# Block 1 attention: VectorE takes the rotations of heads 0 and 1 ahead of recurrences 6 and 7, and the row maxima of head 0 between the two

## The reference, cut to what matters

```
proj = x @ w_in                      # -> x_rnn, g_rnn, q_lat, kv_lat, k_rope, gate_a, gate_b
h_t  = a_t * h_(t-1) + u_t           # RG-LRU over the conv of x_rnn; a, u from its gates
y_rnn = gelu(g_rnn) * h
q    = rms_norm(q_lat) @ w_uq        # 16 heads x (64 plain + 32 rotated)
k, v = rms_norm(kv_lat) @ w_ukv      # k: 64 plain, and 32 rotated, shared by all heads
s    = causal(q k^T / sqrt(96)); p = softmax(s); y_mla = p v
merged = sigmoid(gate_a) * y_rnn + sigmoid(gate_b) * y_mla
x = layer_norm(ALPHA * x + merged @ w_out)
x = layer_norm(ALPHA * x + conv_ffn(x))
```

## Time and profile before

| | us |
|---|---|
| median of 3 runs | 3032.64 |
| lowest, highest | 3029.26, 3034.89 |
| the profiled execution, its own time | 3036.06 |
| its span in the trace | 3034.3 |

### The profile page before, as it was taken

One profiled execution on the slowest core, in us unless ns is written; L12 is line 12 of the kernel. 1 busy time (PEld: TensorE's weight loads), 2 busy tenths in 40 slices (PEclk: granted clock), 3 DMA queues, 4 the chain that ended last, 5 costly groups with the idle time before them and its releaser, 6 DMA issues. The chain is left out here.

```text
span 3034.3 us, 36255 instructions
## 1 busy us (share of the span) xinstructions
PE 2866.3 (94%) x12934; PEld 2256.6 (74%) x12934; DVE 1720.1 (57%) x2416; ACT 1069.9 (35%) x1851; POOL 1540.4 (51%) x929
## 2 busy tenths in 40 slices
PE   8989999999999899999999999889999799899996
PEld 6768787888876687878888876668667566687764
DVE  6865645443137756454442256566777475677775
ACT  3533323221025333332220122534555314444563
POOL 4543356666764533376666654565225253672241
PEclk9999999999999899999999989999999899899998
DMA  4211122333332211123233222125983321246942
GB/s 152 72 63 53 53 75 78 96 96 97 97 97 71 70 56 56 56 77 97 97 97 104 71 91 68 41 91 188 341 320 118 115 70 56 70 169 229 361 166 83
DMA packets 87035, 338.28 MB, mean 111 GB/s; under 512 B 19953, under 2 KB 22769, under 8 KB 77937
## 3 DMA queue, kind: packets, MB, share of 16 engines
q1 hardware_dynamic: 67744, 303.33, 29.4%
q0 software_dynamic: 17280, 26.26, 2.5%
q10 hardware_dynamic: 1872, 6.82, 0.6%
HBM read 371.98 MB, written 30.41 MB: 133 GB/s over the span
## 5 line engine op out<-in xcount | busy, mean ns | idle before, releaser
L179 POOL TENSOR_SCALAR wh<-ring 128x1024 fp32r<-128x1024 f32 x337 | 372.6, 1106 | 1016.7 <-PE ps L240 794.1
L181 POOL TENSOR_TENSOR wl<-ring,wh 128x1024 fp32r<-128x1024 f32 x337 | 827.0, 2454 | 28.1
L238 PE MATMUL ps<-xh,wh 128*128 128x512 f32 x1720 | 697.8, 406 | 32.3 <-POOL xl L439 11.5
L239 PE MATMUL ps<-xl,wh 128*128 128x512 f32 x1720 | 676.1, 393 | 0.0
L240 PE MATMUL ps<-xh,wl 128*128 128x512 f32 x1720 | 676.1, 393 | 0.0
L238 PEld LDWEIGHTS ps<-xh,wh 128*128 128x128 f32 x1720 | 327.3, 190 | 123.5 <-issue 38.2
L239 PEld LDWEIGHTS ps<-xl,wh 128*128 128x128 f32 x1720 | 327.4, 190 | 71.5 <-issue 6.3
L240 PEld LDWEIGHTS ps<-xh,wl 128*128 128x128 f32 x1720 | 326.5, 190 | 70.4
L1434 DVE SCALAR_TENSOR_TENSOR taps<-ps,par,taps 128x511 f32<-128x511 f32 x192 | 143.9, 749 | 237.1 <-ACT taps L1174 221.3
L2793 DVE TENSOR_TENSOR ew_l<-ew,ew_h 128x1024 fp32r<-128x1024 f32 x184 | 219.2, 1251 | 0.0
L2381 ACT ACTIVATE ew_h<-ew 128x1024 fp32r<-128x1024 f32 x184 | 179.3, 1050 | 0.0
(11 more groups left out here) (501 smaller groups left out, 5187.6 us busy)
## 6 DMA issues: line engine op xcount, KB each, us to landing
ring<-in_w SPq DMA_DIRECT2D x343, 512.0 KB, 3.5
ew<-in_eu SPq DMA_DIRECT2D x32, 2048.0 KB, 9.6
ew<-in_ed SPq DMA_DIRECT2D x32, 1024.0 KB, 9.2
yg<-ypicks SPq DMA_DIRECT2D x16, 512.0 KB, 7.0
xrows<-xr ACTq DMA_DIRECT2D x8, 512.0 KB, 2.6
z<-in_x SPq DMA_DIRECT2D x4, 512.0 KB, 4.4
gw<-in_gw SPq DMA_DIRECT2D x2, 1024.0 KB, 6.4
out<-z SPq DMA_DIRECT2D x8, 256.0 KB, 2.9
```

The lines of the kernel that those rows point to most:

```text
L179: nc.gpsimd.tensor_scalar(hi, raw, 1.0, 0.0, ALU.mult, ALU.add).then_inc(sem["w_hi"], 1)
L181: nc.gpsimd.tensor_tensor(lo, raw, hi, ALU.subtract).then_inc(sem["w_split"], 1)
L238: nc.tensor.matmul(out, wh, xh, start=first, stop=False, **kw)
L239: nc.tensor.matmul(out, wh, xl, start=False, stop=False, **kw)
```

## The change

In VectorE's program of each layer of block 1, the two rotations now stand ahead of recurrence 6, and the row maxima of head 0 stand ahead of recurrence 7. No instruction is added, removed or resized.

```diff
                     for p in range(EARLY):
                         recurrence(p)
                         rnn_out(p)
-                    for p in range(EARLY, PAIRS):
-                        recurrence(p)
                     rotate_q(0, 6)
                     rotate_q(1, 5)
+                    recurrence(6)
                     row_max(0)
+                    recurrence(7)
                     rnn_out(6)
                     rnn_out(7)
```

## The result

| | us |
|---|---|
| before, 5 runs | 3031.3 (3028.9 to 3034.89) |
| after, 5 runs | 3014.58 (3013.54 to 3016.39) |
| ratio | 0.9941, 95% interval 0.993 to 0.9951 |
| span of the profiled execution | 3014.6, before 3034.3 |

The change makes the kernel 0.6% faster, 16.7 us between the medians; the interval stands for 15 to 21 us. The forecast was 13.0 us, or 0.9957 of before: the right sign, the time just inside the range, and too small by more than the measurement's uncertainty. The medians leave 3.7 us, the interval 2 to 8 us, that the sum did not have; that is what has to be found.

What follows compares the result with a forecast made beforehand. TensorE, busy 94% of the span, was taken as the bound. Two layers at 7.0 us gave 14.0, less 1.0 for the clock: 13.0 us, from 3032.64 to 3019.6 us, range 3013.5 to 3026.5.

Steps and rivals of the forecast that it cites:

- What the first stall costs: TensorE's 5.68 us idle before scores(0) and the half clock after it: without them scores(1) come 9.3 us earlier per layer.
- Does the rotation come early enough: VectorE's L1330 of head 0 ends at 169.24, so TensorE's wait at scores(0) is gone, with 0.4 us to spare.
- What is late next: row_max(1) starts 2.2 us later than possible, 7.0 earlier than before; second idle grows to 5.4 us; both layers gain 14.0.
- The clock behind the second stall: After TensorE's longer second idle time the clock stays low longer: a loss of 0 to 2.2 us, taken as 1.0.
- From there both engines meet the same instructions in the same relation: Behind TensorE's second idle time everything runs 7.0 us earlier per layer, and the gain stands to the end.
- Rival 1: VectorE's moved instructions keep their old durations: full 9.3 us per layer, 18.5 us gained, 3014.1 us; chance 0.12.
- Rivals 2 to 4: VectorE's chain eats more, gain 5.5 us (0.11); VectorE becomes the bound, 13.4 slower (0.02); scores(0) wait for something else (0.01).

Runs made afterwards that it cites:

- keys_first: Changed kernel with ScalarE copying query 2 and pair 1's keys ahead of head 1's exponentials, first pair of heads only: 3017.38 us, ratio 0.9949 to before.
- the rotations first: Against the changed kernel, row maxima of head 0 moved behind recurrence 7, so both recurrences follow the rotations together: 3021.53 us, ratio 0.9958 to before.
- layer 0 alone: The change made in layer 0 only, layer 1 left as in the kernel before: 3026.87 us, ratio 0.9978 to before.

## Why the prediction was right or wrong

- *What the first stall costs*: right. The forecast was that scores(1) come 9.3 us earlier per layer, and they come 9.2 earlier; the wait is gone, and the clock is 1.00 from 165 to 184.
- *Does the rotation come early enough*: right. L1330 of head 0 was forecast to end at 169.24 and ended at 169.70, 0.4 of it the later start.
- *What is late next*: right. The second idle time was forecast at 5.4 us and is 5.35; scan 7 at 3.3 and is 3.29. The 14.0 us are 14.2.
- *The clock behind the second stall*: wrong, and this is the step that failed. I took 1.0 us as a loss, between 0 and 2.2, on the reasoning that a longer idle time keeps the clock down longer, with a gain left out of the bounds. Measured is a gain, 1.4 to 1.5 us in layer 1, and in layer 0 nothing in one profile and a loss of 0.3 in the other. Two rows of before with the same idle time and lows of 3.04 and 6.44 us already said that the length of the stall is not what sets it; I read them as a spread around the stall's length.
- *From there both engines meet the same instructions in the same relation*: true of the instructions, not of their speed. Another 1.3 us came from the clock in layer 1's norm, 270 us behind the change, and 0.3 behind it. The term was missing.
- With the clock's terms as measured the sum is 14.2 + 1.4 + 1.3 + 0.3 = 17.2 us, against 16.7 and 15.1 between the medians of the two sessions; the medians also hold block 2, which differs by up to 3 us between executions.
- Rival 1 (fixed durations, 18.5 us) gives a time near the measured one, for a reason that the trace refutes: VectorE does reach row_max(1) late. The lower end of my range, 3013.5, stood there for rival 1; my own terms gave 3017 to 3022, with 2 to 3 us more for the spread of a median. That the measured 3014.58 lies inside the range is luck and no support for the clock's term. Rivals 2 to 4 did not occur.

## What to carry to other kernels

When instructions move on an engine that takes turns with another, as VectorE does here with GpSimd, price each by what the other engine does at its new time, not by its old row: here the same scan took 1.2 or 3.3 us. When the critical engine loses one stall, look at everything that it waits for next: taking one of two late inputs away (keys_first) gained nothing, taking both away gained 14.5 us more. And a gain of a few microseconds on TensorE carries a clock term of its own size and of either sign, so give its bounds on both sides of zero, and judge such a variant by timed runs, not by the stall it removes.

## What the runs showed that was not expected

The granted clock behind a stall of one and the same length, 3.2 us, was 0.69, 0.83 to 0.86 or 1.00 over ten microseconds, and within 0.04 the same for a given kernel and layer in seven of the eight places that were seen twice. Shortening a stall from 5.35 to 3.71 us lowered it from 0.85 to 0.69 in one order; lengthening it to 7.53 us lowered it to 0.71. And the clock changed in a stretch 270 us later whose instructions and waits were the same: at layer 1's norm every kernel stood either where before stood (the rotations first, layer 0 alone) or gained 1.5 to 1.7 us (all others), whether it was 5.7 or 29 us ahead when it came there.
